# Products of the identity with itself in front of TensorE's waits, between the projection and the experts of a hybrid decoder layer

## The reference

```
h = rms_norm(x);  P = h @ w_in        # q, k, v of 3 head groups | S5 channels | gate_a | gate_b
A = dilated sliding-window attention of the three groups, merged by softmax denominators
S = S5 state space model (a scan over positions) -> gelu -> y * sigmoid(y @ w_glu + b_glu)
x = x + (sigmoid(gate_a) * (A @ w_a) + sigmoid(gate_b) * (S @ w_s)) @ w_out
x = x + MoE(rms_norm(x))              # router: top 4 of 32 experts; clamped SwiGLU experts
```

## Time and profile before

| | |
|---|---|
| median of 3 runs | 4741.46 us |
| profiled execution | 4742.06 us, its span 4740.4 us, so 1.7 us lie around the span |
| PE busy | 4559.1 us, 96% of the span |
| PEld (weight loads, beside PE) | 3988.5 us, 84% |
| DVE, ACT, POOL busy | 67%, 46%, 20% |
| mean granted TensorE clock | 0.984 of full speed |

### The profile page before, as it was taken

One profiled execution on the slowest core, in us unless ns is written; L12 is line 12 of the kernel. 1 busy time (PEld: TensorE's weight loads), 2 busy tenths in 40 slices (PEclk: granted clock), 3 DMA queues, 4 the chain that ended last, 5 costly groups with the idle time before them and its releaser, 6 DMA issues.

```text
span 4740.4 us, 76690 instructions
## 1 busy us (share of the span) xinstructions
PE 4559.1 (96%) x25756; PEld 3988.5 (84%) x25756; DVE 3161.0 (67%) x6216; ACT 2181.5 (46%) x3608; POOL 931.1 (20%) x911
## 2 busy tenths in 40 slices
PE   8999999999899989997999999999999999999998
PEld 6777787777689978786899999999988888999997
DVE  6668676564556678456555565666667777778887
ACT  4454444343246762232333343343445555556665
POOL 2332101444112001132011111111111111111111
PEclk9999999999999999998999999999999999999999
DMA  6887766555644345543455556565566657777777
GB/s 213 283 311 258 233 202 201 182 164 163 213 163 147 135 160 187 169 145 104 187 180 180 191 169 204 178 209 204 198 210 227 211 208 254 244 245 271 271 268 255
DMA packets 341071, 971.18 MB, mean 205 GB/s; under 512 B 46058, under 2 KB 77589, under 8 KB 303318
## 3 DMA queue, kind: packets, MB, share of 16 engines
q1 hardware_dynamic: 275448, 804.16, 48.0%
q0 software_dynamic: 28304, 88.03, 7.9%
q10 hardware_dynamic: 37085, 76.04, 4.5%
HBM read 772.82 MB, written 200.58 MB: 205 GB/s over the span
## 4 chain that ended last, share of the span: by engine, by line
PE 51%; DVE 1%; ACT 0%; issue 0%; DVEq 0%; POOL 0%; DMA 0%; ACTq 0%; SPq 0%; POOLq 0%
PE ex_d L2802 14%; PE ex_g L2769 11%; PE ex_g L2771 9%; PE ex_g L2765 7%; PE ex_d L2765 4%; PE ex_d L2796 3%; PE ex_d L2771 2%; PE ex_g L2746 1%; PE ex_d L2746 0%; DVE ex_x L2964 0%; PE ex_d L2777 0%; DVEq L2573 0%; ACT ex_wgh L2849 0%; ACT ex_x L2862 0%; DVE ex_y L3038 0%
## 5 line engine op out<-in xcount | busy, mean ns | idle before, releaser
L2771 PE MATMUL ex_g<-ex_x,ex_wgl 128*128 128x256 f32 (+12 forms) x3456 | 980.2, 284 | 0.0
L2769 PE MATMUL ex_g<-ex_x,ex_wgh 128*128 128x288 f32 (+5 forms) x3584 | 755.9, 303 | 1.7 <-DVE ex_x L2964 1.7
L2771 PEld LDWEIGHTS ex_g<-ex_x,ex_wgl 128*128 128x128 f32 x3456 | 652.3, 189 | 3.9
L2946 DVE TENSOR_TENSOR ex_wgl<-ex_wg,ex_wgh 128x2048 fp32r<-128x2048 f32 x274 | 626.6, 2287 | 41.5 <-ACT ex_wgh L2849 41.5
L2849 ACT ACTIVATE ex_wgh<-ex_wg 128x2048 fp32r<-128x2048 f32 x274 | 523.8, 1912 | 280.8 <-PE ex_g L2771 273.9
L2769 PEld LDWEIGHTS ex_g<-ex_x,ex_wgh 128*128 128x128 f32 x3584 | 592.6, 188 | 11.0 <-DVE ex_x L2964 2.1
L2765 PE MATMUL ex_g<-ex_x,ex_wgh 128*128 128x512 f32 (+6 forms) x1664 | 529.4, 376 | 0.9 <-DVE ex_t L2976 0.9
L884 DVE TENSOR_TENSOR prj_wl<-prj_raw,prj_wh 128x512 fp32r<-128x512 f32 x396 | 319.6, 820 | 266.1 <-ACT prj_wh L734 264.9
L681 PE MATMUL prj_p<-prj_wh,prj_ah 128*128 128x512 f32 x1136 | 454.9, 400 | 35.8 <-DVE prj_wl L884 30.4
L2714 POOL DMA_INDIRECT out<-ex_y,ex_cur x82 | 155.5, 1897 | 1501.5 <-ACT ex_y L2870 1243.4
L681 PE MATMUL prj_p<-prj_wl,prj_ah 128*128 128x512 f32 x1136 | 446.6, 393 | 0.0
(11 more groups left out here) (449 smaller groups left out, 9344.6 us busy)
## 6 DMA issues: line engine op xcount, KB each, us to landing
ex_wg<-in_w_gu SPq DMA_DIRECT2D x276, 1024.0 KB, 5.1
ex_wd<-in_w_down SPq DMA_DIRECT2D x276, 512.0 KB, 6.3
prj_raw<-sums_d SPq DMA_DIRECT2D x208, 256.0 KB, 3.0
prj_raw<-in_w_in SPq DMA_DIRECT2D x188, 256.0 KB, 3.2
qkv_d<-prj_o ACTq DMA_DIRECT2D x144, 256.0 KB, 2.5
wo_spare<-qkv_d SPq DMA_DIRECT2D x40, 768.0 KB, 4.2
prj_wt<-in_w_in SPq DMA_DIRECT2D x56, 512.0 KB, 5.8
sums_d<-prj_wt SPq DMA_DIRECT2D x28, 1024.0 KB, 5.3
```

The lines of the kernel that those rows point to most:

```text
L2769: pe.matmul(out[:, 0:size], h[:, k, j, :], x[:, k, 0:size], start=(k == 0 and x is xh), stop=False)
L2771: last = pe.matmul(out[:, 0:size], l[:, k, j, :], xh[:, k, 0:size], start=False, stop=(k == KD - 1))
L2946: tt(flat(wgl[z][:, :, :, :]), flat(wg[r][:, :, :, :]), flat(wgh[z][:, :, :, :]).bitcast(F32), ALU.subtract).then_inc(wgl_ready, 1)
```

## The change

A function `fill(pe, ident, out, n)` issues n plain float32 products of the 128 x 128 identity with itself, none with a semaphore, into a bank that is free at that place. It is called at 14 places, 314 products in all: `s5` 16 at its start, 28 in the first `outputs` before the wait for `st_ready`, 30 at its end; `attention` 12 between the first `turn_q` and `turn_k`, 20 at its end; `mix` 6 at its start, 12 in `turn(1)`, 12 before the first `product`, 28 in `turn(3)`, 36 at its end; `route` 28 at its start, 30 before the last `turn`, 16 before the last `rank`; `experts` 40 before the first transposes, behind the 13 table reads. In `turn(n)` of `mix` the wait for `combined` moves behind the wait for `al_ready` and the products. No other instruction is changed.

```
+def fill(pe, ident, out, n):
+    for _ in range(n):
+        pe.matmul(out, ident[:, :], ident[:, :], start=True, stop=True)
 # s5
                             pe.wait_ge(cpad_in[b % 2], 16 * (b // 2) + 16)
+                            if b == 0:
+                                fill(pe, ident, ps_o[0][:, 0, :], 28)
                             pe.wait_ge(st_ready, b + 1)
+                fill(pe, ident, ps_o[0][:, 0, :], 16)
                 forward(0)
...
                 turn_outputs(NB - 1)
+                fill(pe, ident, ps_t[:, 0, :], 30)
 # attention
                 turn_q(0)
+                fill(pe, ident, sb[0][:, 0, 0:P], 12)
                 turn_k(0)
...
+                pe.wait_ge(s_read, 2 * NU)
+                fill(pe, ident, sb[0][:, 0, 0:P], 20)
 # mix
                 def turn(n):
-                    pe.wait_ge(combined, n + 1)
                     if n >= 2:
                         pe.wait_ge(al_ready, n - 1)
+                    if n in FILLED:
+                        fill(pe, ident, pt[n % 2][:, 0, :], FILLED[n])
+                    pe.wait_ge(combined, n + 1)
+                FILLED = {1: 12, 3: 28}
+                fill(pe, ident, pg[0][:, 0:P], 6)
                 glu(0, range(KA))
                 turn(0)
                 turn(1)
+                fill(pe, ident, po[0][:, 0:P], 12)
                 product(0, 0, 0)
...
+                fill(pe, ident, pt[0][:, 0, :], 36)
 # route
+                fill(pe, ident, po[0][0][:, 0:P], 28)
                 project(0, 0, 0, True)
...
+                pe.wait_ge(h2T_ready, 2 * NT)
+                fill(pe, ident, pt[0][:, 0:P], 30)
                 turn(NT - 1, 1)
                 rank(NT - 2)
                 logits(NT - 1)
+                fill(pe, ident, pt[0][:, 0:P], 16)
                 rank(NT - 1)
 # experts
+                fill(pe, ident, turn_bank(0, None)[:, 0:P], 40)
                 for b in range(B6):
```

4 lines of the change are left out of this document (3 added, 1 removed).

## The result

The changed kernel took 4757.68 us (median of 8 runs, 4751.13 to 4760.01), the kernel before 4741.24 in the same comparison (8 runs, 4738.32 to 4745.79). The ratio is 1.0033, 95% interval [1.0022, 1.0043]: slower by a third of a percent. The profiled execution took 4757.83 us with a span of 4756.2, against 4742.06 and 4740.4 before: +15.8. The mean granted clock rose from 0.984 to 0.989, and TensorE was busy 97% of the span. So the clock was gained as meant, and the time went up.

What follows compares the result with a forecast made beforehand. TensorE, busy 96% of the span, was taken to bound the kernel; fills could win back only half-clock work that others await. Stage terms summed to +11.7 us on 4742.06, giving a median of 4753.2 us, range 4745 to 4760.

Steps and rivals of the forecast that it cites:

- s5 up to SyncE's drain: s5's 16 products at the start count nothing; 28 before the states leave less idling and a warmer clock: -1.1 us.
- attention, start: 12 products between turn_q and turn_k give warm transposes and part of the cold scores back: -1.65 us (-0.5 to -3.25).
- mix, start, quarters and turns: Mix before its end: TensorE idles longer before the third quarter; a clock fall uses up VectorE's slack: +0.3 us (0 to 1).
- mix, fill at the end: 36 products at mix's end last until 1981.2 us against SyncE's 1977.6: +3.7 us.
- route, start: 28 products end before VectorE's last split, which `project` needs; the half clock there cost nothing: 0 us.
- experts, to the first matmul: 40 products behind the 13 table reads, not in the long wait, delay the first expert matmul: +7.5 us (5.3 to 13.2).
- The price of a product: Each fill product is two float32 passes on TensorE: 0.226 us warm, 0.42 us cold.
- The barrier: Stage ends need TensorE drained; fills are free only until SyncE's time: s5 +1.7, attention +0.95, mix +3.7 us.
- turn(3): In mix, 28 products make the transposes 2.4 us late; warm transposes and products win 0.5 and 1.9: 0 us.
- Rival A: All fills: the price of a product is too high, so not slower, 4737 us; chance 0.12.
- rival C: All fills: products of the identity don't keep the clock up, about +55 us, 4797 us; chance 0.04.
- Rival B: Attention, s5 and experts: larger gains, all cold work on the path, 3 us less, 4750 us; chance 0.12.

Runs made afterwards that it cites:

- experiment 10: The kernel before measured once more with no edit: 4738.15 us against 4743.0, ratio 0.9991.
- experiment 9: The changed kernel measured once more with no edit: 4753.65 us against 4743.0, ratio 1.0028.
- experiment 7: Kernel before plus 40 transposes of the identity, in place of 40 products, in front of the experts' transposes; no other fills: 4745.39 us against 4740.69, ratio 1.0011.
- experiment 2: Changed kernel without the fills of 30, 20 and 36 products at the ends of s5, attention and mix: 4750.16 us, ratio 1.0017.
- experiment 1: Changed kernel without the 40 products in front of the experts' transposes, other fills kept: 4749.9 us against 4742.53, ratio 1.0013.
- experiment 11: Changed kernel plus 18 products before the third quarter of mix's first chunk: 4755.17 us against 4743.0, ratio 1.0026.
- experiment 6: Kernel before plus 26 products in front of the experts' transposes, 2 behind each of the 13 table reads: 4744.2 us, ratio 1.0005.
- experiment 3: Kernel before plus only the 40 products in front of the experts' transposes: 4749.03 us, ratio 1.0012.
- experiment 4: Changed kernel, fills cut to their waits, none at route's start or before experts, 18 products added before mix's third quarter: 4738.12 us against 4742.53, ratio 0.9991.
- experiment 8: As experiment 4, but without any fill at the end of mix and in route: 4738.19 us against 4740.69, ratio 0.9992.

## Why the prediction was right

It said slower by over 0.2% with 0.71, 4753.2 us, range 4745 to 4760. The medians were 4757.7 and 4753.7, both inside, the first near the upper end. The ratios, 1.0033 and 1.0028, are both above the 0.2% of the forecast, by about as much as the kernel before differs from itself (0.9991, experiment 10). By its own steps, first against the two profiles of the changed kernel:

| term | forecast | changed | again |
|---|---|---|---|
| s5 up to SyncE's drain | -1.1 | -2.6 | -2.2 |
| s5, fill at the end | +1.7 | +1.6 | +1.6 |
| attention, start | -1.65 | -1.4 | -1.4 |
| attention, fill at the end | +0.95 | +0.7 | +1.0 |
| mix, start, quarters and turns | +0.3 | +2.4 | +2.4 |
| mix, fill at the end | +3.7 | +3.6 | +3.6 |
| route, start | 0 | 0 | 0 |
| route, end | +0.3 | +0.4 | +0.4 |
| experts, to the first matmul | +7.5 | +7.9 | +7.9 |
| sum | +11.7 | +12.6 | +13.3 |

How they are read: at an end, TensorE's drain less SyncE's. For mix it is less the time at which SyncE would have been there, 3.7 us behind the end of VectorE's drain as before, since in the changed kernel SyncE's last store landed 2 us late, and 1 us late in experiment 9 (below). For attention's start it is the matmul after the short or long stall at 163 us, less that stall: 162.1 us before, 160.8 and 160.7 in the changed kernel. That the sum came out within 1 to 2 us is in part luck: s5 is 1.2 to 1.6 us below its two terms and the start of mix 2.1 above. The profiled +15.8 has projection's +3.2 beside this sum, and two differences that cancel: -1.2 in the rest of attention and +1.2 behind the experts' first matmul, of which 0.9 stand behind TensorE's last work.

- **The price of a product** was right: 0.112 us for a pass against 0.113, two passes each, and experiment 7 shows that the passes set the delay. The Trainium skill ("TensorE: Matmul & The Clock Gate", section "Back-to-back issue gap") has about 81 ns for each matmul of 128 columns in a stream, and names no data type for it. For these float32 passes the trace doesn't agree: 112 ns, over 55 spacings in a row.
- **The barrier** waits for the array (experiment 2): the three ends came out within 0.3 us.
- **The experts' fill** stands behind the table reads: right in place and size. That the executions without it lose 1.5 to 2.5 us behind the splits when the clock falls there wasn't seen. It wasn't to be seen in the one profile of before, where it did not fall (experiments 1, 10).
- **Mix, start**: the term that was mis-sized. The prediction named the risk (TensorE idles longer ahead of the third quarter; if the clock falls, VectorE's slack of 1.3 us is used up) and priced it at +0.3, at most 1. The clock did fall, for nearly 7 us, and the transposes came 3.8 us later. From the third quarter's first matmul to them it was 8.1 us (1739.73 to 1747.86) instead of 5.6, which is 2.5 by the clock. The other 1.2 us the quarter itself started late, behind ScalarE's sigmoid, in both profiles of the changed kernel. That sigmoid stands on ScalarE behind a small operation that waits for VectorE, and VectorE there for a load of `att_d`: 2.96 us idle in the changed kernel, 1.61 before, 1.56 in experiment 11. The sigmoid came 11.2 to 11.4 us after the stage's start in both profiles of the changed kernel and in experiment 1, at 10.9 in experiment 2, and at 9.8 to 10.5 in the other nine. Why the load lands later is not shown. Experiment 11 shows 2.2 us of VectorE's time for the two together, with the load early as well. What was off is the size, not the mechanism: with 3.6 us of delay of the transposes taken away, 2.2 came back, so the slack of 1.3 us was right, and the two delays together are three times as long. It isn't the same in every program, though: in experiment 7 the transposes came 2.0 us later than before, and VectorE's drain did not move.
- **turn(3)** at 0: right. With the quarters warm (experiment 11) VectorE drained at 246.6 us against 246.5 before, in spite of the fill's late transposes.
- **Route, start** at 0: right, but with a condition that the prediction did not name, a warm clock ahead of it. Cold, the same fill costs 1.6 us (experiment 2).
- **Attention**: its start was right. The prediction took the rest of the stage as fixed, and it isn't: attention took 389.9 us in the one profile without a long stall and with a cold start (experiment 6), and 392.2 to 394.5 in the four with one stall of about 2 us and a fall of the clock behind it (before, 3, 7, 10). So the stage varies by more than the term.
- **s5**: larger than forecast in these profiles. But the six profiles without the 28 products ahead of the states took 113.2 to 116.3 us, and so the size stays open.

Rival A (a product cheaper) is out by the spacing and experiment 7, rival C (the clock not kept up) by the windows. Rival B's larger gains were in part there in s5, and the start of mix took them back. What stays open is a part of the first median's +16.4: some 4 us above the sum, which the repeat (4753.7, +10.7 against its own before) didn't show again.

**A version that beats both** wasn't found. The fitted fills of experiments 4 and 8 are 15 to 20 us below the changed kernel, and their attention is 4 to 6 us shorter than that of before in the profile. Of that, 1.4 us are the warm start; the rest goes with the long stall, which neither profile has, and experiment 6 had none either without any fill there. Yet their ratios, 0.9991 and 0.9992, are those of the kernel before against itself.

## What to carry to other kernels

A fill that keeps the clock up is free only up to the end of its wait, and a barrier that drains the engine ends that wait earlier than the next stage's first work does. So count a fill in passes of the array, from the first free moment to the earliest thing that could need the engine, and look at what stands ahead of it in program order (here 13 reads, which had eaten the wait). Before filling, ask whether the cold work is on the path: cold transposes in front of other engines' splits cost nothing, and a fill that stops too soon lets the clock fall in a worse place (the end of route in experiment 4, 2 us). Where a gain is two or three us of 4700, compare stages of several profiles, with the unchanged kernel among them; a median here moves by 5 us on its own.

## What the runs showed of the hardware

- The last store of mix landed later in the changed kernel: SyncE waited 3.7 us for it, 1.7 before and in experiment 4. The waits of SyncE over the last 12 us of mix, first of the changed kernel, then of experiment 4:

```profile
SPq L1894 <- DMA mixed_d<-sp_rows: 3.7, 1, 3.7
```

```profile
SPq L1894 <- DMA mixed_d<-sp_rows: 1.7, 1, 1.7
```

In the changed kernel a transfer of 0.02 MB on the queue of instructions stands beside the store, from 5.0 to 3.4 us before the barrier opens, and the last few packets of the store land one by one at 16 GB/s, up to 2 us behind the rest. The same stands in experiment 1 (3.5 us) and in experiment 9 (2.7 us). In the ten other profiles SyncE waited 1.7 us: six have no such transfer in the last 12 us, and four (before, 7, 10 and 11) have it some 11 us before the barrier, clear of the store. It fits a fetch of code that shares a DMA engine with the store; that it is the cause was not tried apart.

- TensorE stalls twice in attention, 161 to 164 us and 196 to 202 us after its start in all programs, for 0.3 to 2.4 us, with "issue" as the only reason told. Which of the two is long repeated in the programs that were profiled twice.
- Reads of a register from the table and matmuls overlap on TensorE: 52 passes between 13 reads took 8.95 us, and the reads without them 7.8 us (2247.5 to 2255.3; experiment 6).
- Forty transposes of the identity raised the clock as 80 passes of products do: it rose 3.4 us after they began, and 3.5 us (experiment 3) and 5.2 us (changed kernel) after the products did. The Trainium skill ("TensorE: Matmul & The Clock Gate", section "Part 4: PE-mode transpose") says that transposes don't bring the full clock; these traces don't agree.
